# Differential-attention layer on one core: the sample tile's projection with high and low parts in one stationary of 128 columns, transposes inside the projection, output stored in halves

## What is computed

```python
h = rms_norm(x, norm_mix)
q, k, v, u, ga, gp = jnp.split(h @ w_in, SPLITS, axis=-1)      # 8 heads of 128
q = rms_norm(q.reshape(b, t, N_HEADS, 2, HEAD_DIM), q_norm)
k = rms_norm(k.reshape(b, t, N_HEADS, 2, HEAD_DIM), k_norm)
o = attention_fn(q, k, v, lam)   # softmax(first half) - lam * softmax(second half), causal
o = (rms_norm(o, head_norm) * (1.0 - lam_init)).reshape(b, t, ATTN_WIDTH)
pool_o, pool_state = pool_mixer(u, pool_prefix, p0, w_pool, pool_scale)
merged = sigmoid(ga) * (o @ w_attn_branch) + sigmoid(gp) * (pool_o @ w_pool_branch)
x1 = x + merged @ w_out
f, ffn_state = conv_ffn(rms_norm(x1, norm_ffn), ffn_prefix, w_up, conv_w, conv_b, w_down)
return x1 + f, ...
```

## Time and profile before

| | |
|---|---|
| median of 3 runs | 2194.64 us |
| profiled execution | 2194.61 us, span 2192.8 us |
| TensorE matmul busy | 2111.4 us, 96% of the span |
| TensorE weight load busy | 1913.0 us, 87% |
| VectorE, ScalarE, GpSimd busy | 48%, 31%, 23% |
| granted TensorE clock, mean | 0.993 of full speed |
| chain that ended last | TensorE 85%, issue 7%, GpSimd 3%, VectorE 2% |
| prologue, heads, phase 2, rest | to 68, 601, 830 and 2192.8 us |

### The profile page before, as it was taken

The page is one execution under the profiler, slowest core; times in us unless marked ns, Lnnn a source line. Parts: engine busy times, 40 slices in busy tenths (PEclk is TensorE's granted clock), DMA queues, the critical chain, the costliest instruction groups (busy, mean ns, idle before and its releaser), DMA issues.

```text
span 2192.8 us, 34549 instructions
## 1 busy us (share of the span) xinstructions
PE 2111.4 (96%) x13557; PEld 1913.0 (87%) x13557; DVE 1060.8 (48%) x1379; ACT 670.5 (31%) x1320; POOL 505.2 (23%) x382
## 2 busy tenths in 40 slices
PE   6999999999999999999999989999999999999998
PEld 6887888888888888799999978999999999899996
DVE  5665575656501010156674343455555555555555
ACT  4444544444434333223212221312211221122120
POOL 5432232322101011143232200212211221122120
PEclk9999999999999999999999999999999999999999
DMA  5121111211267887411223430111101111111112
GB/s 153 51 60 44 53 46 38 59 50 39 64 222 265 276 285 264 130 43 41 68 77 118 127 111 1 49 40 49 60 30 40 49 59 31 40 48 59 30 39 93
DMA packets 174428, 186.28 MB, mean 85 GB/s; under 512 B 8111, under 2 KB 147131, under 8 KB 174274
## 3 DMA queue, kind: packets, MB, share of 16 engines
q1 hardware_dynamic: 163786, 175.21, 25.4%
q10 hardware_dynamic: 10496, 8.92, 1.2%
HBM read 161.09 MB, written 23.24 MB: 84 GB/s over the span
## 4 chain that ended last, share of the span: by engine, by line
PE 85%; issue 7%; POOL 3%; DVE 2%; ACT 1%; DMA 1%; SPq 0%; ACTq 0%; POOLq 0%; DVEq 0%
PE PS L1318 32%; PE PS L1973 12%; PE PS L873 8%; PE PS L268 4%; PE PS L270 4%; PE PS L269 4%; PE PS L1795 3%; PE PS L302 3%; PE PS L326 3%; PE PS L925 3%; PE PS L315 2%; PE PS L940 2%; PE PS L979 1%; POOL fw_lo L1305 1%; PE PS L281 1%
## 5 line engine op out<-in xcount | busy, mean ns | idle before, releaser
L1305 POOL TENSOR_TENSOR fw_lo<-fw_raw,fw_hi 128x1024 fp32r<-128x1024 f32 x86 | 215.2, 2502 | 886.9 <-ACT fw_hi L1301 842.4
L1318 PE MATMUL PS<-m_hi,fw_hi 128*128 128x384 f32 (+1 forms) x1032 | 228.7, 329 | 2.1 <-issue 2.1
L1318 PE MATMUL PS<-m_hi,fw_lo 128*128 128x384 f32 (+1 forms) x1032 | 227.6, 328 | 0.7 <-issue 0.7
L1318 PE MATMUL PS<-m_lo,fw_hi 128*128 128x384 f32 (+1 forms) x1032 | 227.5, 328 | 0.0
L268 PE MATMUL PS<-w_hi,act_hi 128*128 128x384 f32 (+1 forms) x576 | 208.1, 361 | 0.0
L2100 DVE TENSOR_TENSOR x<-x,PS 128x512 f32<-128x512 f32 x198 | 135.9, 688 | 141.0 <-PE PS L1973 141.0
L270 PE MATMUL PS<-w_hi,act_lo 128*128 128x384 f32 (+1 forms) x576 | 195.3, 339 | 0.0
L269 PE MATMUL PS<-w_lo,act_hi 128*128 128x384 f32 (+1 forms) x576 | 194.9, 338 | 0.0
L1318 PEld LDWEIGHTS PS<-m_hi,fw_hi 128*128 128x128 f32 x1032 | 175.8, 188 | 3.4 <-issue 3.0
L1318 PEld LDWEIGHTS PS<-m_hi,fw_lo 128*128 128x128 f32 x1032 | 176.3, 188 | 0.9 <-issue 0.9
L1318 PEld LDWEIGHTS PS<-m_lo,fw_hi 128*128 128x128 f32 x1032 | 176.3, 188 | 0.0
(11 more groups left out here) (254 smaller groups left out, 4131.3 us busy)
## 6 DMA issues: line engine op xcount, KB each, us to landing
k_pg<-in_cache_k_dram SPq DMA_DIRECT2D x64, 512.0 KB, 4.8
v_pg<-in_cache_v_dram SPq DMA_DIRECT2D x64, 512.0 KB, 5.3
fw_raw<-in_w_up_dram SPq DMA_DIRECT2D x44, 512.0 KB, 4.0
fw_raw<-in_w_in_dram SPq DMA_DIRECT2D x24, 512.0 KB, 4.6
wd_raw<-in_w_down_dram SPq DMA_DIRECT2D x22, 512.0 KB, 4.5
w_raw<-in_w_in_dram SPq DMA_DIRECT2D x21, 512.0 KB, 5.2
out_dram<-raw SPq DMA_DIRECT2D x16, 512.0 KB, 3.7
ga_scratch<-ga_ring ACTq DMA_DIRECT2D x8, 544.0 KB, 7.3
```

Source lines behind the costliest of these rows:

```text
L1305: e.tensor_tensor(fw_lo[slot][:, 0:kts, :], fw_raw[:, 0:kts, :], fw_hi[slot][:, 0:kts, :].bitcast(F32), ALU.subtract).then_inc(fw_tail, 1)
L1318: ins = e.matmul(PS[:, 3 * slot + c, 0:cw], w[slot][:, kt, :], x[:, kt, c0:c0 + cw], start=first and kt == 0, stop=last and kt == KT - 1)
```

## The change

For the sample tile, high and low parts of the 64 tokens lie side by side in a new tile `both` (7 k-tiles of 128 columns, made in the prologue). With it as stationary operand, one matmul against the high weights and one against the low weights give high x high and high x low in partitions 0 to 63 of the bank, low x high (and low x low) in partitions 64 to 127. The last k-tile stays with three matmuls of 64 columns, and it is issued second. ScalarE copies the lower half into raw, and VectorE adds the upper half (`dve_add_upper`) and then frees the bank. Space comes from qT and kT (1024 columns where they had 1088) and from osb, which holds four blocks where it held eight and is stored twice per head. At s = 8 the q transposes and the first group go inside the projection before its fourth k-tile, the k transposes and the second group before its sixth. ScalarE's copies are put in the same order. The first scores of a head no longer wait for the copy of the last output.

```diff
+    PAIRS = KT - 1
+    both = r("both", [P, PAIRS, 2 * NSAMP], F32R)
-            for kt in range(KT):
-                if kt in between:
-                    between[kt]()
+            for i in range(KT):
+                kt = i
+                if s == QT:
+                    kt = 0 if i == 0 else KT - 1 if i == 1 else i - 1
+                if i in between:
+                    between[i]()
...
+                if s == QT and kt < PAIRS:
+                    out = PS[:, bank, 0:3 * VD]
+                    e.matmul(out, both[:, kt, :], h3, start=kt == 0, stop=False)
+                    ins = e.matmul(out, both[:, kt, :], l3, start=False, stop=kt == PAIRS - 1)
+                    continue
...
         def pe_scores(e, h, slot, s):
             if s == 0:
-                e.wait_ge(b7_free, FIRST_USES + h * USES_PER)
+                e.wait_ge(b7_free, FIRST_USES - 1 + h * USES_PER)
...
                 if s == QT:
-                    q_part()
-                    matmuls({5: k_part})
-                    first_group()
-                    second_group()
+                    matmuls({3: q_and_first, 5: k_and_second})
                 elif s < 5:
-                    q_part()
-                    matmuls({2: first_group, 5: k_part})
+                    matmuls({2: first_and_q, 5: k_part})
...
+                e.wait_ge(pj_free, n * TT + 2)
             e.wait_ge(pj_full, n * TT + s + 1)
             e.activation(raw[slot][0:rows(s), s, :], PS[0:rows(s), PJ + (slot + s) % 2, 0:3 * VD],
-                         ACT.Copy).then_inc(pj_free, 1)
+                         ACT.Copy).then_inc(lower_copied if s == QT else pj_free, 1)
...
+                    if s == QT // 2 + 1:
+                        e.wait_ge(o_st[0], h * 16 + 16)
                     e.wait_ge(b7_full, use + 1)
-                    e.activation(osb[:, s - 1, :], PS[:, B_O, 0:VD], ACT.Copy).then_inc(b7_free, 1)
-            e.wait_ge(b7_free, use + 1)
-            e.dma_start(o_dram[0:SEQ, bass.ds(h * VD, VD)].rearrange("(t p) d -> p t d", p=P),
-                        osb[:, :, :]).then_inc(o_st, 16)
+                    e.activation(osb[:, (s - 1) % (QT // 2), :], PS[:, B_O, 0:VD], ACT.Copy).then_inc(b7_free, 1)
+                if s in (QT // 2, QT):
+                    half = s // (QT // 2) - 1
+                    e.wait_ge(b7_free, use + 1)
+                    e.dma_start(o_dram[half * SEQ // 2:(half + 1) * SEQ // 2, bass.ds(h * VD, VD)]
+                                .rearrange("(t p) d -> p t d", p=P), osb[:, :, :]).then_inc(o_st[half], 16)
...
+        def dve_add_upper(e, n, slot):
+
+            e.wait_ge(lower_copied, n + 1)
+            dst = raw[slot][0:NSAMP, QT, :]
+            e.tensor_tensor(dst, dst, PS[NSAMP:2 * NSAMP, PJ + (slot + QT) % 2, 0:3 * VD], ALU.add).then_inc(pj_free, 1)
```

More of the change, by code:

```diff
@@ L132, in build_step @@
     raw = [r(f"raw{i}", [P, TT, 3 * VD]) for i in range(2)]
-    qT = [r(f"qT{i}", [P, TOK]) for i in range(2)]
-    kT = [r(f"kT{i}", [P, TOK]) for i in range(2)]
+    qT = [r(f"qT{i}", [P, SEQ]) for i in range(2)]
+    kT = [r(f"kT{i}", [P, SEQ]) for i in range(2)]
     e_at = r.at
@@ L139, in build_step @@
     osb_at = r.at
-    osb = r("osb", [P, QT, VD])
+    osb = r("osb", [P, QT // 2, VD])
     sq = r("sq", [P, 3, 2 * VD])
+    PAIRS = KT - 1
+    both = r("both", [P, PAIRS, 2 * NSAMP], F32R)
     pgt_at = X_END - fit(NB * NPG)
@@ L197, in build_step @@
         kv_st = [sem(f"kv_st{i}") for i in range(2)]
-        o_st = sem("o_st")
+        o_st = [sem(f"o_st{i}") for i in range(2)]
         class Step:
@@ L269, in pe_project @@
                 e.matmul(out, a_hi, l3, start=False, stop=False)
-                ins = e.matmul(out, a_lo, h3, start=False, stop=kt == KT - 1)
+                ins = e.matmul(out, a_lo, h3, start=False, stop=s < QT and kt == KT - 1)
             ins.then_inc(pj_full, 1)
@@ L414, in act_evac_qk @@
                 e.wait_ge(b7_full, use + part + 1)
-                w = 3 * P if g < 2 else 2 * P + NSAMP
+                w = 3 * P if g < 2 else 2 * P
                 if g < 2:
@@ L456, in take_matmuls @@
                         act_chunk(e, s)
[L458 to L461, removed]
+                if group and s == QT:
+                    act_evac_qk(e, *group, parts=(0,))
                 if s >= 1:
@@ L465, in act_head @@
                     act_evac_qk(e, *group, parts=(0,))
+                if group and s == QT:
+                    act_evac_qk(e, *group, parts=(1,))
                 if s >= 5:
@@ L498, in act_phase1 @@
                     e.wait_ge(tr_x, 2 * t + half + 1)
+                    if t == QT:
+                        k0, k1 = 4 * half, min(4 * half + 4, PAIRS)
+                        e.activation(both[:, k0:k1, 0:NSAMP], PS[:, 2 * (t % 2) + half, 0:(k1 - k0) * P]
+                                     .rearrange("p (a b) -> p a b", b=P)[:, :, 0:NSAMP], ACT.Copy)
                     e.activation(act_hi[:, 4 * half:4 * half + 4, t * P:t * P + rows(t)],
@@ L532, in dve_tail_x @@
                 src = PS[:, 2 * (t % 2) + half, :].rearrange("p (a b) -> p a b", b=P)[:, :, 0:rows(t)]
+                if t == QT:
+                    k0, k1 = 4 * half, min(4 * half + 4, PAIRS)
+                    e.tensor_tensor(both[:, k0:k1, NSAMP:2 * NSAMP], src[:, 0:k1 - k0, :],
+                                    both[:, k0:k1, 0:NSAMP].bitcast(F32), ALU.subtract)
                 e.tensor_tensor(act_lo[:, 4 * half:4 * half + 4, t * P:t * P + rows(t)], src,
@@ L582, in dve_head @@
                     dve_scale_qk(e, h + 1, 1 - slot, s // 3 - 1)
+                if proj and s == QT:
+                    dve_add_upper(e, h + 1, 1 - slot)
         DVE_HEAD = 4 * QT + 3
@@ L683, in pool_constants @@
                 e.sem_inc(s, 2 + N_U)
[L686 removed]
+            for s in (kv_st[0], kv_st[1], o_st[1], os_st[0], os_st[1], st_st, os_full, os_copied, pt_free,
                       exp_done, pts_copied):
```

31 lines of the change are left out of this document (22 added, 9 removed).

## The result

| | before | after |
|---|---|---|
| median of 4 runs each, same chip | 2194.55 us (2193.65 to 2196.14) | 2160.89 us (2159.43 to 2162.38) |
| ratio | | 0.9846, interval 0.9829 to 0.9863 |
| span of the profiled execution | 2192.8 us | 2160.6 us |
| TensorE matmul busy | 2111.4 us | 2096.9 us |
| TensorE's first scores; last values of phase 1 | 68.30; 598.83 us | 67.09; 570.19 us |

What follows compares the result with a forecast made beforehand. The prediction took TensorE's in-order list as the bound (85% of the chain that ended last). Its terms, 18.1 + 2.5 + 1.4 + 0.2 - 0.5 = 21.7 us off 2194.6, gave 2172.9 us, range 2168.6 to 2178.5.

Steps and rivals of the forecast that it cites:

- The matmul term: Sample tile's projection: 24 matmuls become 17, seven fewer at 0.173 us each, 1.21 us saved per projection.
- the rival with 7.1 us less: Loads set the pace in the 128-column matmuls: 0.19 us saved per projection instead of 1.21, time 2180; chance 0.05.
- The block: s = 8, values 6 to values 7, heads 0 to 6: 6.17 us against 8.75, 18.1 us saved in seven heads.
- The three thin margins: s = 8 block: probabilities and ScalarE's copies ready 0.17, 0.1 and 0.2 us before TensorE needs them, so no wait returns.
- The last head: Last head's s = 8 block, with gate chunks for a projection: 7.69 to 6.26 us, 1.4 saved, bounds 1.1 and 1.6.
- The half store: osb's first half lands before ScalarE's copy at s = 5, costing nothing; rival: landing after 7.6 us stops ScalarE, chance 0.02.
- The waits move: Rival: matmuls go, but waits of about 1.1 us per head move rather than vanish, time 2181.6; chance 0.06.
- at the two loop-backs ... no gain taken, up to 0.3 each: TensorE stands 3.38 us at "issue" there, osb copy long done: no gain counted, up to 0.3 us each possible.
- the head start: Next head's scores no longer wait for the last output copy: 2.5 us saved in five places, bounds 2.1 and 2.6.
- a clock drop: Half clock after head 0's longer wait: price 1.2 to 1.5 us, chance about 0.4, 0.5 us charged.
- a rival of mine, put at s = 8: GpSimd stretches VectorE's probabilities of block 7, first transpose group waits about 1.1 us per head, time 2180.6; chance 0.05.
- Behind the heads: Start of phase 2: ScalarE's 3.26 us wait for the last store shortens, 0.2 us saved, bounds 0 and 0.8.

Runs made afterwards that it cites:

- e2: Kernel before, without the low x high matmuls of seven of the sample tile's eight k-tiles, waits and order unchanged; 2183.5 us.
- e12: e10 with the old order of s = 8 on TensorE and ScalarE, paired matmuls kept; 2171.31 us.
- e6: Kernel before with 128 increments of an unused semaphore at the start of TensorE's program; 2186.58 us.
- e7: Changed kernel with 64 increments of an unused semaphore at the start of TensorE's program; 2171.37 us.
- e5: Kernel before with TensorE's loop of heads written out, other engines keeping theirs; 2183.73 us against 2196.07.
- e9: Kernel before with 133 unused-semaphore increments ahead of TensorE's loop of heads (70 at the start, 63 in the prologue's projections); 2183.42 us.
- e10: Changed kernel with 133 unused-semaphore increments ahead of TensorE's loop of heads (70 at the start, 63 in the prologue's projections); 2160.64 us.
- e8: Changed kernel with the q and k transposes of s = 2 put back in front of the projection; 2164.65 us.
- e4: Changed kernel with ScalarE's first weight split of a head moved behind the exponentials and the raw copy of s = 0; 2161.94 us.
- e11: e10 with ScalarE's first weight split moved behind the exponentials of position 0, as in e4; 2156.0 us.
- e1: Changed kernel with 16 instructions added ahead of TensorE's loop (tile 0's transposes made twice); 2163.54 us.
- e3: Changed kernel with the first scores of a head again waiting for the last copy into osb; 2165.34 us.

## Why the forecast was too small

**Right.** The matmul term was 7 x 0.173 = 1.21: e2 measured 1.21 and e12 1.20. Loads don't set the pace (the rival with 7.1 us less). Those of 128 columns take 189 ns, as in the earlier trace rows, and the matmuls start 0.173 to 0.175 us apart all the same. The block was forecast at 6.17 us and is 6.06, by two errors that partly cancel: each insertion of transposes takes 0.68 us (194.06 to 194.74) where 0.83 was reckoned, and the 17 matmuls take 3.22 where 3.03 was. The three thin margins held: nothing waits inside the block. The scores of a head come 0.5 to 0.57 us sooner (forecast 0.5, bounds 0.42 to 0.52). The last head gave 1.6 for 1.4. VectorE's addition takes 0.56 us and no one waits for it. The half store lands in 2.3 us, once in 5.5, where the rival began at 7.6, so that it had nothing behind it. "The waits move" is refuted by the list above.

**The step that failed: "at the two loop-backs ... no gain taken, up to 0.3 each".** I read 3.38 us of "issue" as a fixed price of a loop-back. It was the fetch of instructions, and it hung on where the loop's code lies (e6, e7), which the change had shifted and shortened. It gave 5.5 of the 6.6 us at the two branches (the rest is the head start there), and 0.9 more behind them, where before stood at half clock (1.2 of 2.4 GHz) for 3.4 us each. Those 3.4 us cost 0.4 to 0.5 only, since a later wait for GpSimd swallowed part: position 0 of head 4 took 6.36 us for 4.81, position 2 7.15 for 8.03 in head 1. Two rows would have told me to ask: the branch's own duration, 3.8 and 4.1 us taken against 0.08 not taken, and 117 instruction packets. e5 and e9, the old kernel with quick branches, give the price without any of the change: 6.8 and 6.4 us less in heads 1 to 6. For the change against an equal base, 22.8 us remain, 1.1 more than the forecast. That nearness is partly luck, since errors of both signs are in it: head 0 gave nothing, and what lies behind the heads went 2.9 us the other way. The range, too, left out at its lower end the 1 us either way that it allowed at the other; 26.0 plus 1 would still have missed 33.7. ("Fifteen 2.69 us less" in the first paragraph should read: fifteen take 2.69 us.)

**A part not costed.** The diff also moves the q transposes of s = 2, and at 4.0 us in five waits for GpSimd's gain they stood in the view that I read for the earlier trace rows. I took only the rows that the text of the change named. In their place stands a wait of 0.34 us for VectorE's probabilities (149.38 in head 1; the same in four other heads, 0.17 in one). Net 0.2 to 0.4 us a head, 1.7 in six from e9 to e10; e8 shows the wait come back. With the 0.9 behind the loop-backs these are the 2.6 of the table.

**Head 0, mis-sized.** Forecast: wait 1.55 growing to 2.8 us, ended at 74.7, a clock drop charged at 0.5. Measured, TensorE in the changed kernel:

```profile
75.60 0.70 PE L313 MATMUL PS<-kT,qT 64*128 64x256 f32 x4 [3.64 <-ACT E L455]
```

and ScalarE in front of it:

```profile
73.69 1.16 ACT L419 ACTIVATE w_hi<-w_raw 128x1152 fp32r<-128x1152 f32 x1 [5.91 <-DMA w_raw<-in_w_in_dram]
```

The load landed 0.9 us later than in the earlier trace rows, where I had it fixed at 72.79; TensorE was ready 1.2 us sooner; 1.55 + 1.2 + 0.9 = 3.65. e2, the old kernel with nothing but matmuls left out, bears this out: its wait there is 2.8 us (1.55 before), half clock follows for 6.8 us, and the rest of head 0 takes 60.61 us (56.51 before, 61.56 after). Then the rest (window, busy time of each engine, granted clock):

```profile
77.00:80.00 3.00, 1.88 (x7) 1.38 (x6) 2.96 (x3) 0.28 (x1) 1.89 (x1) 0.50 0.00 0
80.00:84.00 4.00, 4.00 (x15) 4.00 (x15) 3.61 (x7) 1.02 (x4) 1.82 (x1) 0.55 0.02 4
```

Half clock from 76.8 to 83.6 costs up to 3.4 us, and the probabilities, which the change didn't move, met GpSimd's weight tail and took 2.81 us for 0.35:

```profile
76.22 2.81 DVE L603 SCALAR_TENSOR_TENSOR E<-E,rden 128x128 f32<-128x128 f32 x1
```

TensorE waited 1.12 us for that. I had priced the drop at 1.2 to 1.5 us with a chance of 0.4. That VectorE would be stretched was a rival of mine, put at s = 8, where it did not happen. e4 and e11 show that the wait comes from the order on ScalarE: with the split behind the exponentials it is gone (3.64 us, then 0.2 at most). Head 0 is then 66.8 us long in both, 0.1 to 2.7 less than the 66.9 to 69.5 of the versions with the old order, so that what it gives back isn't settled.

**Behind the heads.** Forecast 0.2, measured 3.6. ScalarE's wait for the last store falls from 3.26 to 2.40 us, 0.9 of the gain, and does the same from e9 to e10. Half clock at the start of phase 2 falls from 6.8 to 3.4 us, by estimate up to 1.7 more. But e10 takes 2.9 us more behind the heads than e9, so nothing beyond the 0.9 is shown to be the change's. The rest I leave open: where half clock falls in the long stretch behind the heads wasn't followed, and that stretch takes from 1584.2 (e6) to 1594.0 us (before) over all the profiles.

**What stays open.** Close to a multiple of 256 the count of blocks doesn't decide. With branches at 2298 to 2316 (the edge is at 2304), e1 was quick twice, e2 slow twice, and e3, e4 and e8 had one of each, in one execution of one code. The changed kernel itself, at 2300, was quick twice in its profile. e2 and e3 have their loops at the same place (646 to 2298) and differ in the waits, so near an edge something beside the place takes part. In the channel mixer branches at 16626 to 16644 (edge at 16640) were slow but for one of 18, and a loop that begins 17 short of an edge and touches eight (e5) was quick.

The packets say what the cases near an edge have in common. From the start to the loop's first branch, in before (to 200.7 us), e1 (to 195.9), e2 (to 201.7) and e6 (to 205.2):

```profile
q8 instruction: 9, 0.15, 0.3%
```
```profile
q8 instruction: 8, 0.13, 0.3%
```
```profile
q8 instruction: 9, 0.15, 0.3%
```
```profile
q8 instruction: 9, 0.15, 0.3%
```

Among the loops that begin in the third block of 256, at 646 to 710, every branch with 8 packets ahead of it was quick (the changed kernel, e1, the first of e3, e4 and e8), and every one with a ninth was slow (before, e2, e7, the second of e4 and e8), but for the second of e3, which was slow and got its ninth 0.8 us after it began. In before the ninth starts at 200.40, 0.33 us ahead of the branch. Where the loop begins one block later (e6, e9 to e12), nine packets go with quick branches. In the channel mixer of e2 there are 9 packets from its first branch to the second, which was slow, and 8 from there to the third, which was quick. So the traces fit this: a branch is slow once a block has been fetched that is the ninth, counted from the loop's first. The channel mixer's loop of e5 is the one exception, nine by this count and quick, and no run was made to test it. What lets the ninth come early with the branch at 2298 and keeps it away at 2316 stays open.

So the gain from quick branches in phase 1 isn't safe: 64 instructions more ahead of the loop take it away (e7). And of the 10.9 us between 33.7 and 22.8 the profiles place 6.4 in heads 1 to 6 and 6.5 behind the heads, with 2.4 the other way at the start and in head 0; no run isolates the 6.5.

## What to carry to other kernels

Where TensorE idles at "issue" behind a loop's end, look at the duration of its branch (0.2 against 3.3 to 4.8 us here) and at the instruction queue's packets in each pass; moving the same body, with none of its work changed, was worth 9.5 us here (e6). So compare a change with a base whose loops lie equally, or the loop's gain is booked to the change. And cost every wait in the view that the diff touches, not only those that the change is named for; where a stage opens with a load, ask when that load lands, since time saved ahead of it is given back and the idle engine may restart at half clock.

## What the runs showed of the hardware that I had not expected

- A taken branch of TensorE cost 0.21 to 0.25 us or 3.3 to 4.8 us. A slow branch brings 9 packets of 16 KB each time. With the branch 36 instructions or more past an edge, loops of 1647 to 1680 instructions that touch seven blocks of 256 were quick (e6, e9 to e12), those that touch eight slow (before, e7), in phase 1 and in the channel mixer alike; e5's in the channel mixer, eight and quick, is the exception. What goes with the slow branches is a ninth block fetched, counted from the loop's first.
- A slow branch is exposed in part only: 1.9 to 2.9 us of it at a head's end, 1.0 to 1.4 us in the channel mixer's passes.
- 128 increments of a semaphore start 0.15 us apart on TensorE's sequencer, and its first transposes come at 20.49 us where they came at 9.77 (e6). With 70 of them and 63 spread over the prologue, the first scores came 0.4 (e10) and 1.0 us (e9) later.
- VectorE beside one GpSimd operation of 2.6 us: 3.40 for 0.95 us (128 x 768), 2.81 for 0.35 (128 x 128). The expectation of e11 also has 1.92 for 0.42; that is no such case, since the 0.42 belongs to another shape (128 x 384), and the operation of 128 x 256 takes 1.61 to 1.92 us in all eight heads of e4.
- Stores of 512 KB from ScalarE's queue landed in 3.2 us at best, of 256 KB in 2.3 (15 of 16, one in 5.5).
